# Expert slots of 64 rows with plain fp32 products for seven of sixteen experts in one layer of a diffusion backbone

## The reference

```python
def moe_ffn(h, w_router, b_router, w_gate, w_up, w_down):
    ...
    aff = jax.nn.sigmoid((tok @ w_router).astype(jnp.float32))
    # the best of 4 groups of 4 experts, and in it the best two; their weights sum to 1
    ...
    counts = jnp.bincount(flat_e, length=N_EXPERTS)
    padded = (counts + EXPERT_BLOCK - 1) // EXPERT_BLOCK * EXPERT_BLOCK
    ...
    def expert_block(args):
        xb, e = args                                   # 128 rows of 1024
        hb = jax.nn.silu(xb @ w_gate[e]) * (xb @ w_up[e])
        return hb @ w_down[e]                          # three 1024 x 1024 matrices per expert
```

## Time and profile before

| | |
|---|---|
| device time, median of 3 runs | 2021.61 us (2019.91 to 2021.72) |
| span of the profiled execution | 2016.2 us, so 5.4 us of the median lie outside of such a span |
| PE busy | 1964.6 us, 97% |
| DVE busy | 1717.3 us, 85% |
| ACT busy | 1162.6 us, 58% |
| DMA | 629.45 MB, 312 GB/s over the span, 390 to 406 in most slices of the two expert stages |
| chain that ended last | PE 83%, DVE 9%, DMA 5% |
| expert stage, layer 0 / layer 1 | about 564 to 1117 us / 1446 to 1997 us |

### The profile page before, as it was taken

One profiled execution on the slowest core, in us unless ns is written; L12 is line 12 of the kernel. 1 busy time (PEld: TensorE's weight loads), 2 busy tenths in 40 slices (PEclk: granted clock), 3 DMA queues, 4 the chain that ended last, 5 costly groups with the idle time before them and its releaser, 6 DMA issues.

```text
span 2016.2 us, 25838 instructions
## 1 busy us (share of the span) xinstructions
PE 1964.6 (97%) x9392; PEld 1566.4 (78%) x9392; DVE 1717.3 (85%) x1731; ACT 1162.6 (58%) x1134; POOL 196.5 (10%) x254
## 2 busy tenths in 40 slices
PE   7999999999999999999999998999999999999996
PEld 3788558778888888888888577677888888888885
DVE  4775789898689999999999988777799999999997
ACT  2324613323367777777777355344477777777774
POOL 3000110111030000000000300100100000000001
PEclk9999999999999999999999999999999999999998
DMA  9766417666489999999999677286799999999995
GB/s 347 269 238 224 143 67 240 244 221 252 183 284 410 391 406 392 397 392 398 396 400 390 250 254 250 64 328 222 271 391 390 399 395 397 391 403 387 405 388 219
DMA packets 181489, 629.45 MB, mean 312 GB/s; under 512 B 13903, under 2 KB 16091, under 8 KB 174368
## 3 DMA queue, kind: packets, MB, share of 16 engines
q1 hardware_dynamic: 150648, 503.62, 66.1%
q0 software_dynamic: 27808, 119.98, 16.2%
q10 hardware_dynamic: 2952, 4.77, 0.6%
HBM read 597.13 MB, written 31.19 MB: 312 GB/s over the span
## 4 chain that ended last, share of the span: by engine, by line
PE 83%; DVE 9%; DMA 5%; ACT 2%; issue 1%; SPq 1%; POOL 0%; ACTq 0%; DVEq 0%; POOLq 0%
PE bank L2517 78%; PE bank L2527 4%; DVE work L1693 3%; DMA ring<-in_w_mod_dram 1%; DVE m_lo L1693 1%; DVE ring L1693 1%; PE bank L2790 1%; DMA ring<-in_w_in_dram 1%; DMA work<-hp_dram 1%; DMA ring<-in_w_exp_down_dram 1%; DVE work L2073 1%; DVE w_lo L1693 1%; DMA x<-in_ctx_dram 1%; DMA ring<-in_w_out_dram 1%; ACT work L1444 0%
## 5 line engine op out<-in xcount | busy, mean ns | idle before, releaser
L1693 DVE TENSOR_TENSOR w_lo<-ring,w_hi 128x2048 fp32r<-128x2048 f32 x384 | 873.6, 2289 | 87.8 <-ACT w_hi L1556 86.2
L1556 ACT ACTIVATE w_hi<-ring 128x2048 fp32r<-128x2048 f32 x384 | 738.0, 1922 | 237.1 <-PE bank L2517 232.1
L2517 PE MATMUL bank<-w_hi,xsT_hi 128*128 128x512 f32 x1024 | 399.8, 390 | 0.8 <-DVE w_lo L1693 0.6
L2517 PE MATMUL bank<-w_lo,xsT_hi 128*128 128x512 f32 x1024 | 398.6, 389 | 0.0
L2517 PE MATMUL bank<-w_hi,xsT_lo 128*128 128x512 f32 x1024 | 315.4, 389 | 0.0
L1276 ACT ACTIVATE m_hi<-ring 128x1024 fp32r<-128x1024 f32 (+1 forms) x128 | 129.8, 1031 | 262.2 <-PE bank L2517 211.9
L2517 PEld LDWEIGHTS bank<-w_hi,xsT_hi 128*128 128x128 f32 x1024 | 192.2, 188 | 44.9 <-issue 1.9
L2517 PEld LDWEIGHTS bank<-w_hi,xsT_lo 128*128 128x128 f32 x1024 | 192.2, 188 | 40.2
L2517 PEld LDWEIGHTS bank<-w_lo,xsT_hi 128*128 128x128 f32 x1024 | 192.2, 188 | 38.6
L2517 PE MATMUL bank<-w_hi,hexpT_hi 128*128 128x512 f32 x512 | 202.3, 395 | 0.6 <-DVE w_lo L1693 0.6
L2517 PE MATMUL bank<-w_lo,hexpT_hi 128*128 128x512 f32 x512 | 199.5, 390 | 0.0
(11 more groups left out here) (304 smaller groups left out, 2634.5 us busy)
## 6 DMA issues: line engine op xcount, KB each, us to landing
ring<-in_w_exp_gate_dram SPq DMA_DIRECT2D x128, 1024.0 KB, 9.1
ring<-in_w_exp_up_dram SPq DMA_DIRECT2D x128, 1024.0 KB, 7.9
ring<-in_w_exp_down_dram SPq DMA_DIRECT2D x128, 1024.0 KB, 8.6
ring<-in_w_in_dram SPq DMA_DIRECT2D x44, 1024.0 KB, 7.3
work<-in_w_mod_dram POOLq DMA_DIRECT2D x40, 1024.0 KB, 5.6
ys_dram<-work POOLq DMA_DIRECT2D x32, 512.0 KB, 7.8
work<-hp_dram SPq DMA_DIRECT2D x54, 256.0 KB, 4.4
work<-mod_dram POOLq DMA_DIRECT2D x8, 1024.0 KB, 9.5
```

The source lines that it names most:

```text
L1556: nc.scalar.activation(w_hi[:, pos % N_SPLIT, :], raw(i), ACT.Copy).then_inc(hi_done, 1)
L1693: return nc.vector.tensor_tensor(o, a, b, op)
L2517: return nc.tensor.matmul(o, a, b, start=first, stop=last)
```

## The change

`KINDS` gives each of the 16 slots of a layer a kind: W (wide, as before) or N (narrow). Layer 0 is all W. Layer 1 is WW, then NW seven times: slots 2, 4, ... 14 are narrow.

- **Ranking on the chip.** In both layers DVE sorts the experts by their number of rows. Experts 0, 1 and 15 keep fixed slots; the 13 others go by rank, in layer 1 the seven with the fewest rows to the narrow slots. SP reads each slot's expert number from `of_rank` before it loads that expert, and POOL's place numbers count by rank.
- **A narrow slot** has 64 places. Its 64 rows are gathered as 128 half rows of 512 numbers (`idx_few`, two more index loads), so the lower 64 partitions hold the first halves, the upper the second. Four transposes turn them at once, ACT copies once, nothing is split. The products are plain fp32 ones on the raw slot: the two halves of the output columns stand in two column tiles of the array, 64 columns each, and in one bank. PE waits for the load itself, and the slot is free when PE has used it. Silu, the product of gate and up, and the copy to ys are one operation each instead of two; the store is two of 64 rows by 512 numbers.
- **If a narrow expert had over 64 rows**, or a wide one over 128, the extra path would open (`most` counts 64 more for the narrow ones).
- **Loops are written out** on all engines.
- **Moves.** The place numbers stood ahead of quarter 1's split; now they follow the ranking, as two pieces in the row of `shares`.

```diff
+FEW = 64
+KINDS = ["W" * 16, "WW" + "NW" * 6 + "NW"]
+FIXED = {0: 0, 1: 1, NE - 1: 2}
...
+def wide_quarter(l, n):
+    e, p = ((n + 4) // PER_EXPERT, (n + 4) % PER_EXPERT) if n >= 8 else (0, n)
+    return wide(l, e if e < NE and p < 8 else e - 1)
...
+                def expert_in(e):
+
+                    if e not in stands:
+                        if len(stands) == len(FIXED):
+                            sp.wait_ge(routed, 5 * l + 1)
+                        r = rank_at(l, e)
+                        stands[e] = sp.value_load(of_rank[0:1, r:r + 1], min_val=0, max_val=NE - 1)
+                    return stands[e]
+
+                def free_after(n):
+
+                    if wide_quarter(l, n):
+                        return lo_done, splits_before(l, n) + 1
+                    return w_used, used_after(l, n)
...
-                turn(0)
-                turn(1)
-                with sp.Fori(2, NE) as e:
-                    turn(e)
+                for e in range(NE):
+                    for p in range(turns(e)):
+                        load(e, p)
...
                 pool.dma_start(idx_exp[:, :], first_rows).then_inc(idx_loaded, 16)
-                pool.wait_ge(idx_loaded, 16 * (l + 1))
+                for half in range(2):
+                    pool.dma_start(idx_few[FEW * half:FEW * (half + 1), :], first_rows[0:FEW, :]).then_inc(idx_loaded, 16)
+                pool.wait_ge(idx_loaded, 48 * (l + 1))
...
+                        else:
+                            pool.wait_ge(routed, 5 * l + 5)
+                            pool.indirect_dma_start(xs[:, e % 2, 0:CH], None, h2_halves,
+                                                    bass.IndirectOffsetOnAxis(ap=idx_few[:, r:r + 1], axis=0))\
+                                .then_inc(xs_loaded[e % 2], 16)
...
+                def ranks():
+                    ...
+                    link(nc.vector.scalar_tensor_tensor(out=key, in0=rows_in, scalar=float(NE),
+                                                        in1=const[:, K_ORD:K_END], op0=ALU.mult, op1=ALU.add))
+                    link(TT(wins, along(key), across(key), ALU.is_gt))
+                    link(nc.vector.tensor_reduce(rank, wins, AX.X, ALU.add))
+                    link(TT(wins, along(rank), across(iota), ALU.is_equal))
+                    link(TT(wins, wins, along(iota), ALU.mult))
+                    link(nc.vector.tensor_reduce(held, wins, AX.X, ALU.add))
+                    nc.vector.tensor_copy(of_rank[:, :], held).then_inc(routed, 1)
+                    ...
+                    yield
+                    ...
...
+                        if (e, p) == (1, 2):
+                            dve.wait_ge(idx_loaded, 48 * (l + 1))
+                            nc.vector.tensor_scalar(idx_few[:, :], idx_few[:, :], 2.0, upper, ALU.mult, ALU.add)\
+                                .then_inc(routed, 1)
...
-                expert(0, 0, shares())
-                for e in range(1, 4):
+                expert(0, 0, itertools.chain(ranks(), shares()))
+                for e in range(1, NE):
                     expert(e, e % 2)
...
+                def product_few(b, few, e, p, par):
+
+                    n0 = stream(e, p)
+                    i = n0 % N_RAW
+                    pe.wait_ge(slot_loaded[i], 16 * (base_loads[l][i] + n0 // N_RAW + 1))
+                    for k in range(2):
+                        kk = 2 * (p % 4) + k
+                        for n in range(2):
+                            rows = slice(FEW * n, FEW * (n + 1))
+                            ins = nc.tensor.matmul(b[rows, :], few[:, par, kk % 4, kk // 4, :],
+                                                   raw(i)[:, k * D + n * CH:k * D + (n + 1) * CH], start=kk == 0,
+                                                   stop=kk == KB - 1, tile_position=(0, FEW * n))
+                    ins.then_inc(w_used, 1)
```

More of the change, by code:

```diff
@@ L90, in early_blocks, with wide, rank_at, banks_before @@
     return [tb for tb in tokens_of(l) if l + 1 == DEPTH or tb in tokens_of(l + 1)]
+def wide(l, e):
+    return KINDS[l][e] == "W"
+def rank_at(l, e):
+    if e in FIXED:
+        return FIXED[e]
+    ahead = sum(1 for i in range(e) if i not in FIXED and wide(l, i) == wide(l, e))
+    return ahead + (len(FIXED) if wide(l, e) else KINDS[l].count("W"))
+def banks_before(l, e):
+    return sum(2 if wide(i, k) else 1 for i in range(l + 1) for k in range(e if i == l else NE))
+def wide_before(l, e):
+    return sum(2 for i in range(l + 1) for k in range(e if i == l else NE) if wide(i, k))
+def stream(e, p):
+    if e == NE:
+        return PER_LAYER - PER_EXPERT + p
+    return PER_EXPERT * e - 4 + p if e else p
+def wide_quarter(l, n):
+    e, p = ((n + 4) // PER_EXPERT, (n + 4) % PER_EXPERT) if n >= 8 else (0, n)
+    return wide(l, e if e < NE and p < 8 else e - 1)
+def splits_before(l, n):
+    return sum(wide_quarter(i, k) for i in range(l + 1) for k in range(n if i == l else PER_LAYER))
+def used_after(l, n):
+    return l * PER_LAYER + n + 1
+def stored_through(l, e):
+    return sum(16 if wide(i, k) else 32 for i in range(l + 1) for k in range(e % 2, e + 1 if i == l else NE, 2))
 GOT_EARLY = [1, 3]
@@ L1607, in expert @@
                             gate(e)
-                        if isinstance(e, int) and e == 0:
+                        if e == 0:
                             if p == 5:
@@ L1623, in _ @@
                 take_xs(0, 0)
[L1624 to L1630 removed]
+                for e in range(NE):
+                    expert(e, e % 2)
                 high(NE, 10)
@@ L3005, in gate_up @@
                     for p in range(8):
                         up = p // 4
-                        if first and p == 5:
+                        if e == 0 and p == 5:
                             turn_xs(1, 1)
-                        if second and p == 4:
+                        if e == 1 and p == 4:
                             turn_h(0)
                             turn_last()
-                        product((bank[2 + up], bank[4 + up]), xsT_hi, xsT_lo, e, p, par)
+                        if wide(l, e):
+                            product((bank[2 + up], bank[4 + up]), xsT_hi, xsT_lo, e, p, par)
+                        else:
+                            product_few(bank[2 + up], xsT_few, e, p, par)
```

381 lines of the change are left out of this document (218 added, 163 removed).

## The result

The changed kernel takes 2031.45 us, median of 4 runs (2027.75 to 2033.01), against 2021.66 for the kernel before in 4 runs beside it: ratio 1.0047, 95% interval 1.0035 to 1.0059. The forecast was 2004 us with a range up to 2022, so both the sign and the range were wrong.

The account below looks back on a forecast made before the run. TensorE was taken as the bound, DMA 3 to 4% behind. Terms -26 + 5.6 + 4.0 + 0.5 = -16, and -1, gave -17: span 2016.2 to 1999, with 5.4 around it 2004 us; range 1991 to 2022.

Parts of the forecast that it names:

- seven pairs, first narrow expert: Layer 1: each narrow expert with its wide neighbour 65.2 us instead of 68.9, -26; first narrow expert finds full slots, -1.
- ranking, layer 0: Head of layer 0: VectorE's ranking delays w_lo of the first expert's quarters 3 to 7, so TensorE waits, 5.6 us.
- ranking, layer 1: Head of layer 1: ranking delays w_lo by the same steps, 4.0 us, bounds 0 and 9.
- index wait, layer 0: Layer 0, expert 1: VectorE waits for the later index load, splits for TensorE behind it, 0.5 us, bounds 0 and 4.
- code without loops: All engines: writing the loops out was taken to cost 0.
- does the queue stay full?: Layer 1 joints: TensorE's delay is made up within each pair; two of six slots stay in flight, enough for 410 GB/s.
- 4: Rival, layer 1: joints cost more than narrow experts give back, VectorE in order behind h and ys; 2018 us, chance 0.12.
- 1: Rival, layer 1: the DMA queue gives no more than its mean of 395 GB/s; 2023 us, chance 0.10.
- 2: Rival, narrow products: pairs of 64-column tiles stand in line, 3.44 us a quarter; 2086 us, chance 0.08.
- 3: Rival, narrow experts: TensorE's clock falls in their gaps, quarters of 3.6 us; at least 2100 us, chance 0.04.
- pairs of 68 us: Sign of being wrong, layer 1: a narrow expert with its wide neighbour takes 68 us or more.
- the clock did leave 1.00 after 1500 us: Sign of being wrong: TensorE's clock leaves 1.00 after 1500 us.

Follow-up runs that it names:

- e4: Changed kernel without any ranking, layer 0 as before, layer 1's seven narrow experts chosen beforehand: 2015.5 us.
- e1: Changed kernel with all experts wide, no ranking and no narrow index, only the code without loops left: 2028.0 us, ratio 1.0025.
- e9: Changed kernel without the narrow index load and VectorE's wait for it in layer 0, ranking kept in both layers: 2023.5 us, ratio 1.0010.
- e3: Changed kernel with layer 0 as before (no ranking, no narrow index, no wait for it), layer 1 as in the change: 2018.8 us, ratio 0.9981.
- e2: Changed kernel with all experts wide in both layers, ranking kept, no narrow index load or wait: 2034.9 us.
- e6: Kernel e3 with narrow products reading a constant block instead of loaded weights, each narrow slot free once landed: 2004.0 us.
- e7: Kernel e3 with layer 1's ranking cut into four pieces instead of two: 2021.6 us, ratio 0.9997.
- e5: Kernel e3 with 18 dummy products ahead of each wide down projection that follows a narrow gate and up: 2022.0 us.
- e8: Kernel e3 with layer 1's order two wide, seven narrow, seven wide: 2011.0 us, ratio 0.9942.
- e11: Kernel e8 with ten narrow experts instead of seven (two wide, ten narrow, four wide): 2006.4 us, ratio 0.9918.

## Why the prediction was wrong

Term by term, us of the profiled stages:

```
term                              forecast   measured            from
seven pairs, first narrow expert  -26 - 1    -13.8               e4 - e1, layer 1
ranking, layer 0                  +5.6       +4.2 to +5.1        e9 - e3; e2 - e1
ranking, layer 1                  +4.0       +3.4 to +4.4        e2 - e1; e3 - e4
index wait, layer 0               +0.5       +6.4                changed - e9
code without loops                 0         +5.4 (span)         e1 - before
```

Measured, the terms sum to 5.6 to 7.5 us, of the 9.8 by which the medians differ; the rest isn't attributed.

1. **The pairs, the largest miss.** The step "does the queue stay full?" failed. It counted "about two loaded slots more" held by PE and called the two of six in flight "just enough". They weren't: the rate fell to 342 to 362 GB/s for 16 us in the pair shown, and -27 became -13.8. The rate itself was forecast rightly (410), and so was what a pair would take at it: with the slots free on landing (e6) it takes 65.9, and -13.8 - 10.9 = -24.7 stands beside the forecast's -27. The bounds of that term (-8 to -41) held what came. No row stood behind the count of slots.
2. **The index wait.** The forecast placed the index at 603 and the DVE's arrival at 603, and concluded 0.5 us, at most 4. DVE was there at 604.3; the index came at 611.5, because POOL took 26.7 us from the first scatter to the load instead of the 20.2 of the earlier trace rows, and began 1.9 us later than supposed. Two late numbers were set against each other as if both were exact, and behind the wait stood everything that PE needs. With its clock at 0.50 after it, 7.2 us of waiting cost 6.4.
3. **Loops.** "Unrolled loops: 0" was written without a row. e1 shows some 5 us (3 to 7) in the medians.
4. **The heads' ranking** was sized nearly right in both layers (5.6 and 4.0; by the medians of e2 and e1 6.9 instead of 9.6). Whether its order in the first expert matters stays open, since e7 brought a wait of its own.
5. **The rest** of the 12.8 us of span, 3.6 between the stages and 1.2 ahead of the first beyond what e1 has there, is no more than kernels with equal code differ by in those stretches. The 5.4 us that the sum adds for what lies around the span are mostly a fast execution under the trace; since the sum goes from median to median with them, they did no harm.

The rivals: 4 (joints cost more than narrow experts give back) named the right place and nearly the size, +2 us a pair where 2.3 were lost, but another mechanism: DVE in order behind h and ys, where the runs show slots held by PE; and alone that would still have been faster than before. 1 gave the right number for the pair (67.7 us at 395 GB/s, against 67.5) by the wrong cause: in e6 the queue gave 406. 2 is refuted by the 1.8 us quarter, 3 by e5, e8 and e11. Of the signs of being wrong, pairs of 68 us never came (67.5), while the clock did leave 1.00 after 1500 us, and e5 found no price for it. The slower sign is none of them: it is the sum of a halved gain, an index wait and the loops, each of which the text had priced at its favourable end.

## What to carry to other kernels

Ask of each buffer who frees it: an edit that lets TensorE read a loaded slot directly moves the slot's release from a fast early reader to the bound engine, and the transfers pay for that whenever this engine is behind. Light and heavy pieces that share a ring are then better put in groups than in alternation (here 0.9942 instead of 0.9981 of the time before, one line). And a cheap small operation that waits for a far result must not stand in an in-order queue that feeds the bound engine, least of all in a stage that doesn't use the result.

## What the hardware showed that was not expected

- Two 64-column tiles of plain fp32 products of 512 columns cost what one costs: a quarter of four products in 1.8 us (x16 in 3.65).
- With TensorE 77 to 81% busy in short gaps the clock was 0.97 to 1.00 in each 50 us from 1550 to 1800 us of e11. A gap of 5.0 us in the changed kernel (1609 to 1614), behind 8 us in which it was busy for 4.6, was followed by 0.50 (1614 to 1618). Yet holding the clock at 1.00 won nothing (e5).
- A core's DMA queues gave 410 GB/s in each 50 us from 1550 to 1850 us of e11. The 424 of the highest 2.5 us in the earlier trace rows didn't last: in no trace here did 50 us pass 412.
- The same program without loops took about 5 us more of 2020, with 26 more instruction packets; the cause is open.
